# DeltaNet values: SiLU on VectorE six steps later, their block transpose five steps later

## The reference, cut to what matters

```python
qkv_c = jax.nn.silu(causal_depthwise_conv(qkv, conv_w))
q, k, v = jnp.split(qkv_c, 3, axis=-1)
q = l2_normalize(heads(q))
k = l2_normalize(heads(k))
...
a_low = jnp.where(strict, jnp.einsum("bhnid,bhnjd->bhnij", k_beta, k) * gamma, 0.0)
rhs = jnp.concatenate([v * beta, k_beta * jnp.exp(decay)[..., None]], axis=-1)
sol = lax.linalg.triangular_solve(a_low + jnp.eye(CHUNK, dtype=f32), rhs, ...)
qk = jnp.einsum("bhnid,bhnjd->bhnij", q, k) * gamma
```

## Time and profile before

| | us |
|---|---|
| median of three runs | 1756.55 |
| lowest and highest | 1755.61, 1759.47 |
| the profiled execution | 1757.64 |
| its span, first to last instruction | 1755.6 |

### The profile page before, as it was taken

How to read it: one execution, slowest core, us unless ns; L and a number is a source line. 1 busy time by engine, 2 the same in 40 slices (tenths; PEclk the granted TensorE clock), 3 DMA queues, 4 the chain that set the end, 5 groups by cost and what they waited for, 6 DMA issues and landing times.

```text
span 1755.6 us, 26154 instructions
## 1 busy us (share of the span) xinstructions
PE 1733.2 (99%) x9690; PEld 1403.6 (80%) x9690; DVE 1307.9 (75%) x1926; ACT 877.0 (50%) x1403; POOL 107.1 (6%) x82
## 2 busy tenths in 40 slices
PE   9999999999999999999999999999999999999998
PEld 7877777777777888888888888888888888888886
DVE  5788898998976688875777796888644468886444
ACT  6665555655644555454444455444433344444443
POOL 0030040220300000000000000000000000000000
PEclk9999999999999999999999999999999999999999
DMA  8676767766756677766666665555555555556554
GB/s 290 203 218 193 216 211 213 219 210 211 213 178 195 199 237 238 222 190 195 207 204 204 203 216 192 193 191 191 194 193 196 194 185 193 195 195 194 193 193 142
DMA packets 125416, 356.34 MB, mean 203 GB/s; under 512 B 13968, under 2 KB 42784, under 8 KB 125184
## 3 DMA queue, kind: packets, MB, share of 16 engines
q1 hardware_dynamic: 123568, 350.80, 62.8%
q0 software_dynamic: 880, 3.24, 0.6%
q10 hardware_dynamic: 864, 0.87, 0.2%
HBM read 332.84 MB, written 22.02 MB: 202 GB/s over the span
## 4 chain that ended last, share of the span: by engine, by line
PE 80%; DVE 9%; issue 7%; DMA 2%; SPq 1%; ACT 1%; POOL 0%; POOLq 0%; ACTq 0%
PE acc L536 26%; PE acc L538 25%; PE acc L537 25%; DVE w_lo L1400 4%; DVE cT L1430 2%; DVE qn L1436 1%; PE J L633 1%; DMA bounce<-rawg 1%; PE J L759 1%; DMA og_hi<-bounce 1%; SPq L414 1%; PE J L643 0%; PE J L769 0%; DMA raw<-weights 0%; PE J L703 0%
## 5 line engine op out<-in xcount | busy, mean ns | idle before, releaser
L1400 DVE TENSOR_TENSOR w_lo<-raw,w_hi 128x1024 fp32r<-128x1024 f32 x582 | 721.1, 1245 | 310.9 <-ACT w_hi L960 307.8
L960 ACT ACTIVATE w_hi<-raw 128x1024 fp32r<-128x1024 f32 x582 | 614.7, 1059 | 675.7 <-PE acc L538 650.5
L536 PE MATMUL acc<-w_hi,hT_hi 128*128 128x512 f32 x1432 | 572.6, 400 | 11.6 <-DVE w_lo L1400 11.6
L537 PE MATMUL acc<-w_lo,hT_hi 128*128 128x512 f32 x1432 | 559.2, 390 | 0.0
L538 PE MATMUL acc<-w_hi,hT_lo 128*128 128x512 f32 x1432 | 558.3, 390 | 0.0
L536 PEld LDWEIGHTS acc<-w_hi,hT_hi 128*128 128x128 f32 x1432 | 268.8, 188 | 82.2 <-DVE w_lo L1400 17.4
L538 PEld LDWEIGHTS acc<-w_hi,hT_lo 128*128 128x128 f32 x1432 | 269.1, 188 | 57.4
L537 PEld LDWEIGHTS acc<-w_lo,hT_hi 128*128 128x128 f32 x1432 | 269.2, 188 | 52.9 <-issue 1.0
L536 PE MATMUL acc<-w_hi,act_hi 128*128 128x512 f32 x512 | 199.2, 389 | 0.0
L537 PE MATMUL acc<-w_lo,act_hi 128*128 128x512 f32 x512 | 199.2, 389 | 0.0
L538 PE MATMUL acc<-w_hi,act_lo 128*128 128x512 f32 x512 | 199.2, 389 | 0.0
(11 more groups left out here) (252 smaller groups left out, 1365.9 us busy)
## 6 DMA issues: line engine op xcount, KB each, us to landing
raw<-weights SPq DMA_DIRECT2D x582, 512.0 KB, 3.5
bounce<-rawg SPq DMA_DIRECT2D x12, 512.0 KB, 5.0
og_hi<-bounce SPq DMA_DIRECT2D x64, 64.0 KB, 3.7
p_bounce<-prob SPq DMA_DIRECT2D x7, 512.0 KB, 4.8
keyed<-p_bounce SPq DMA_DIRECT2D x28, 128.0 KB, 5.6
og_lo<-bounce SPq DMA_DIRECT2D x32, 64.0 KB, 3.6
k_bounce<-rawg SPq DMA_DIRECT2D x4, 512.0 KB, 5.5
xres<-k_bounce SPq DMA_DIRECT2D x16, 128.0 KB, 4.1
```

Of the source, the lines that this page charges most:

```text
L536: mm(o, aT_hi[:, kt, tok], w_hi[:, c % RING, w], start=first, stop=False)
L537: mm(o, aT_hi[:, kt, tok], w_lo[:, c % RING, w], start=False, stop=False)
L960: A(w_hi[:, slot], raw[:, slot], ACT.Copy).then_inc(hi_ready, 1)
L1400: tt(w_lo[:, slot], raw[:, slot], w_hi[:, slot].bitcast(F32), ALU.subtract).then_inc(lo_ready, 1)
```

## The change

Two numbers of the table that sets VectorE's order. The same instructions are issued on the same data.

```diff
-DVE_SILU = {ITEM_K: -17, ITEM_Q: -5, ITEM_V: 5}
-DVE_BACK = {ITEM_K: -16, ITEM_Q: -3, ITEM_V: 8}
+DVE_SILU = {ITEM_K: -17, ITEM_Q: -5, ITEM_V: 11}
+DVE_BACK = {ITEM_K: -16, ITEM_Q: -3, ITEM_V: 13}
```

## The result

The changed kernel takes 1762.27 us in the median of seven runs (1761.78 to 1767.55) against 1756.66 of the kernel before: a ratio of 1.0033 with a 95% interval of 1.0024 to 1.0042, or some 5.6 us more. The forecast was 1763.6.

What follows compares the result with a forecast made beforehand. TensorE, busy 99% of the span, was taken to bound the kernel. Four groups, each 1.77 us later with the 0.28 gain already taken off, add 7.1 us to the median 1756.55, giving 1763.6; range 1758.0 to 1768.5.

Steps and rivals of the forecast that it cites:

- SiLU gone from step 5: VectorE ahead of the block L1532: the block starts 0.28 us sooner, the other 3.0 us become idle time.
- third wait: TensorE's last of three waits per head group for VectorE's low half of a weight chunk, 0.46 us; to shorten by 0.28.
- Transpose gone from step 8: VectorE ahead of product L1554: removing its 1.23 us gives nothing, since L1554 waits for TensorE's q k^T matmuls.
- SiLU added at step 11: Between L1554 and add L1443, beside GpSimd's mask product: SiLU stands still for GpSimd and is over at about 252.7.
- Hand-over: TensorE and VectorE alternate on the triangular inverse (`spread`, add, `square`, masked copies); TensorE becomes 1.77 us later per group.
- Transpose added at step 13: Behind the masked copies, ahead of the next add: its 1.23 us cost nothing, covered by 0.90 idle and later slack.
- Queue behind: SyncE's write of the values waits for the transpose; it lands at 262.7, the read back is not late, by 0.6 us.
- Relief: First rival: the whole 0.61 us of the third wait goes in each group, 2.4 us faster, 1754.1; chance 0.06.
- SiLU at its bare time: Second rival: at step 11 GpSimd's mask product gives way or comes later, so SiLU is not blocked: 1758.3; chance 0.14.
- The third rival: TensorE's new wait ahead of `square` lets its clock fall, 1.6 us, once to four times: 1765.2 to 1770.0; chance 0.14.

Runs made afterwards that it cites:

- experiment 2: Against the kernel before, SiLU of the values moved from step 5 to step 8 and the transpose from 8 to 13: ratio 0.9994, 1756.11 against 1758.02 us.
- experiment 3: SiLU at step 10, one step earlier than in the changed kernel, transpose at 13: ratio 0.9994 to the kernel before, 1756.39 us.
- experiment 1: Against the kernel before, only the transpose moved, from step 8 to 13, SiLU staying at step 5: ratio 0.9997, 1757.61 against 1758.02 us.
- experiment 4: The changed kernel with GpSimd's mask product of the third level held until the second add: ratio 1.0011 to the kernel before, 1760.03 against 1758.02 us.
- the second timing: The changed kernel itself timed and profiled again, nothing altered: ratio 1.0038 to the kernel before, 1765.22 us.
- experiment 5: SiLU at step 12, between the first add with its low half and the masked copies, transpose at 13: ratio 1.0023 to the kernel before, 1762.43 against 1758.37 us.
- experiment 6: The changed kernel with the transpose one step earlier, at 12, ahead of the first masked copies: ratio 1.0053 to the kernel before, 1768.06 us.
- experiment 8: Against the kernel before, SiLU of the values to step 8, their transpose to 13, q's transpose from step -3 to 5 with its dependents: ratio 1.0003.

## Why the prediction was right

Point by point, by its own steps.

- **SiLU gone from step 5.** Forecast: 0.28 gained, the other 3.0 idle time. Measured: third wait shorter by 0.30, VectorE idle for 2.4 us, and its low half there 0.5 longer. Right, and experiments 2 and 3 keep this gain.
- **Transpose gone from step 8.** Forecast: nothing, since L1554 waits for TensorE. In the changed kernel L1554 idles 1.21 for it, and experiment 1 has the old time. Right.
- **SiLU added at step 11.** Forecast 2.66 us (250.04 to 252.70), measured 2.44 from its start to the add. That it is blocked by GpSimd is shown by experiment 4, which takes GpSimd away and gets 1.42 back. The term was too high by 0.2: the second instruction starts at 250.67 and the third at 252.10, 1.43 later, of which 1.1 are standing still; the forecast had the full 1.31 of GpSimd's operation there. Its rule, that an instruction stands still until GpSimd's operation is over and then runs in full, asks a little too much.
- **Hand-over.** `spread` to `square` 3.89 (4.16 forecast), `square` to `spread` 3.12 (3.12 forecast). Net per group 1.48 for 1.77: 0.2 are SiLU's, the rest is the slack of `square`, 0.76 where the sum had 0.71, and roundings. For four groups that is 5.9 for 7.1, 1.2 us less, and it explains the miss of 1.3 us in the first timing; the second timing gave 6.7 us, which lies between 5.9 and 7.1. One sentence of the prediction, that TensorE has no slack for this add, is wrong by this; its sum used the slack all the same. Experiments 3 and 5 place the cost: a step ahead of the hand-over SiLU is free, and one later it costs the same kind of wait at the other end.
- **Transpose added at step 13.** Forecast: nothing. Experiment 1 shows it, experiment 6 what it costs without its cover, 1.12 in the trace for 1.23.
- **Queue behind.** The write was seen at 257.78 and the read back at 263.35, forecast 257.6 and 263.3. The write landed in 2.6 us and not in 5.0; the 0.6 us of slack was larger.
- **Rivals.** Relief alone is out, since `square` waits. SiLU at its bare time is what experiment 4 makes: 1.9 us, forecast 1.8. The third rival had the price of a fall, 1.6 us, but took it from a fall which itself cost nothing, and it had the wrong place: the clock fell behind the old second wait and behind a late transfer, never behind the new wait of 1.61 in the twelve groups of the three profiles with it. That a longer wait brings a fall is not borne out either: 1.77 us had one in some groups and 2.79 had none.

## What to carry to other kernels

A step may be moved for free only to where its engine idles for another. Look for the row with idle time ahead of it and put the step in front of that row; the next row may be the one for which the busiest engine waits. There, count what it has to spare: of SiLU's 2.44 us the first 0.76 were free. Count the neighbour that can hold the moved work up too: here GpSimd made 1.34 us of work into 2.5, and in experiment 8 it ate the time that had been freed.

## What the runs showed of the hardware

- VectorE's instructions with two SBUF inputs stood still for GpSimd's operations in every place where they met: SiLU's 1.34 us became 3.30 (before, two operations) and 2.44 (step 11, one), and where it met none (steps 8, 10 and 12, and experiment 4) its four instructions took their bare 1.42 from the first start to the last end. The price of one operation was somewhat less than its 1.3 us: 1.1 at step 11. It goes the other way too: behind the first SiLU instruction GpSimd's operation took 1.48 us instead of 1.31. The Trainium skill, "SBUF — State Buffer", section "SBUF: two separate sides", says that of such two the one that starts first goes ahead and the other waits, and the traces agree, but for the somewhat lower price.
- The block transpose, with one input, took 1.23 to 1.25 beside GpSimd and alone. VectorE's add L1443, with one input in SBUF and one in PSUM, took 0.69 us beside GpSimd's 1.30 (257.78 in the changed kernel) and 0.67 without it (252.77).
- The granted clock fell to 1.2 GHz behind waits of 1.77 to 2.33 us in some groups of one execution and not behind equal waits in others, nor behind the longest, 2.79; the new waits of 1.61 had no fall. A fall costs up to 1.6 us; that of the earlier trace rows cost nothing, as the next wait ended 4.78 us behind the last one, as in the other groups: VectorE was the later one there anyway. What decides it these runs leave open.
